# Second block: probabilities turned in 32x32 blocks too, turned operands kept in blocks of their own order, the three score units in one granule

## The reference

```
h = x @ w_in                          # q, k, v, z for 12 heads A and 12 heads B of 128, gates g
qa, ka = rope(qa), rope(ka)
out_a = mixture of three dilated causal windows over q, k, v (heads A)
out_b = softmax(q k' / sqrt(128) + D_t - D_s, causal) v      (heads B; D: summed log forget gates)
y = sigmoid(g_a) * ((out_a * silu(za)) @ w_up_a) + sigmoid(g_b) * ((out_b * silu(zb)) @ w_up_b)
x = layer_norm(x * alpha + y @ w_out)
```

## Time and profile before

| | |
|---|---|
| runs, median of 3 | 2801.91 us (2800.36 to 2802.63) |
| profiled execution | 2799.75 us |
| its span | 2798.0 us |
| mean granted TensorE clock | 0.994 |
| TensorE products / its weight loads | busy 99% / 81% of the span |
| VectorE, ScalarE, POOL | busy 65%, 48%, 13% |

### The profile page before, as it was taken

The page is one execution under the profiler, slowest core; times in us unless marked ns, Lnnn a source line. Parts: engine busy times, 40 slices in busy tenths (PEclk is TensorE's granted clock), DMA queues, the critical chain, the costliest instruction groups (busy, mean ns, idle before and its releaser), DMA issues.

```text
span 2798.0 us, 35964 instructions
## 1 busy us (share of the span) xinstructions
PE 2757.6 (99%) x13157; PEld 2253.2 (81%) x13157; DVE 1817.0 (65%) x2220; ACT 1346.3 (48%) x1765; POOL 370.9 (13%) x653
## 2 busy tenths in 40 slices
PE   8899999999999999999999999999999999999998
PEld 5477887888888888888888888888888888888886
DVE  7889899778657556655555556575565545555565
ACT  3255646556544453544444544444445444445443
POOL 0000010000001223100133100022131011331000
PEclk9999999999999999999999999999999999999999
DMA  9987798865655566566566566565566665665554
GB/s 397 414 311 241 272 342 307 309 222 190 215 194 181 188 201 205 185 220 196 191 202 203 191 196 223 181 195 187 191 203 205 208 199 183 206 206 187 193 213 148
DMA packets 178617, 622.74 MB, mean 223 GB/s; under 512 B 27688, under 2 KB 27984, under 8 KB 173088
## 3 DMA queue, kind: packets, MB, share of 16 engines
q1 hardware_dynamic: 155376, 583.08, 60.3%
q0 software_dynamic: 23088, 37.56, 4.6%
HBM read 599.51 MB, written 2.14 MB: 215 GB/s over the span
## 4 chain that ended last, share of the span: by engine, by line
PE 90%; DMA 4%; DVE 4%; ACT 1%; issue 0%; SPq 0%; DVEq 0%; ACTq 0%
PE acc L860 65%; PE acc L2455 16%; DMA raw<-in_w 2%; DVE wlo L1865 1%; PE psS L839 1%; PE psS L829 1%; DMA scr<-in_w_early 1%; PE psS L2455 1%; PE psS L2421 1%; PE psT L812 1%; PE psT L2378 1%; DMA mraw<-in_w_early 1%; DVE raw L1900 0%; PE psS L2440 0%; PE psT L2340 0%
## 5 line engine op out<-in xcount | busy, mean ns | idle before, releaser
L489 DVE TENSOR_TENSOR wlo<-raw,whi 128x1024 fp32r<-128x1024 f32 x670 | 819.4, 1224 | 783.7 <-ACT whi L372 782.0
L372 ACT ACTIVATE whi<-raw 128x1024 fp32r<-128x1024 f32 x670 | 708.9, 1059 | 980.3 <-PE acc L860 964.4
L860 PE MATMUL acc<-whi,tokens_hi 128*128 128x512 f32 x2304 | 632.3, 395 | 0.5 <-DVE tokens_lo L303 0.3
L860 PE MATMUL acc<-whi,tokens_lo 128*128 128x512 f32 x2304 | 618.2, 389 | 0.0
L860 PE MATMUL acc<-wlo,tokens_hi 128*128 128x512 f32 x2304 | 618.1, 389 | 0.0
L860 PEld LDWEIGHTS acc<-whi,tokens_lo 128*128 128x128 f32 x2304 | 432.4, 188 | 91.5
L860 PEld LDWEIGHTS acc<-wlo,tokens_hi 128*128 128x128 f32 x2304 | 432.4, 188 | 91.0
L860 PEld LDWEIGHTS acc<-whi,tokens_hi 128*128 128x128 f32 x2304 | 425.7, 188 | 85.6 <-DVE tokens_lo L303 0.9
L1564 ACT ACTIVATE whi<-raw 128x1024 fp32r<-128x1024 f32 x160 | 168.7, 1058 | 200.8 <-PE acc L2455 116.2
L1865 DVE TENSOR_TENSOR wlo<-raw,whi 128x1024 fp32r<-128x1024 f32 x160 | 195.3, 1223 | 82.2 <-ACT whi L1564 81.3
L2455 PE MATMUL acc<-whi,tokens_hi 128*128 128x512 f32 x800 | 226.1, 403 | 1.9 <-DVE tokens_lo L1974 1.2
(11 more groups left out here) (355 smaller groups left out, 2434.2 us busy)
## 6 DMA issues: line engine op xcount, KB each, us to landing
raw<-in_w SPq DMA_DIRECT2D x838, 512.0 KB, 4.2
raw<-in_w_late SPq DMA_DIRECT2D x80, 512.0 KB, 5.0
mraw<-in_w SPq DMA_DIRECT2D x64, 512.0 KB, 4.7
mraw<-in_w_late SPq DMA_DIRECT2D x48, 512.0 KB, 4.8
y<-in_w_early SPq DMA_DIRECT2D x12, 1024.0 KB, 15.4
mraw<-in_w_early SPq DMA_DIRECT2D x7, 1024.0 KB, 14.9
scr<-in_w_early SPq DMA_DIRECT2D x7, 1024.0 KB, 14.8
sgl<-in_w_early SPq DMA_DIRECT2D x6, 1024.0 KB, 15.0
```

Of the source, the lines that this page charges most:

```text
L372: act.activation(whi[:, n % SLOTS, :], raw[:, n % SLOTS, :], ACT.Copy).then_inc(s_hi, 1)
L489: dve.tensor_tensor(wlo[:, n % SLOTS, :], raw[:, n % SLOTS, :], whi[:, n % SLOTS, :].bitcast(F32), ALU.subtract).then_inc(s_lo, 1)
L860: m = pe.matmul(acc[c % 2][:, tb, :], a[:, kk, tb * P:(tb + 1) * P], b[:, n % SLOTS, k * CW:(k + 1) * CW], start=(kk == 0 and q == 0), sto ...
```

## The change

What it does:

- The `p` fills and their copies go. In step 33 (`R_PROB`) VectorE turns all 1536 columns of `prob` in 32x32 blocks into `pb`, which lies in the joint tile of `qT` and `kT`; POOL moves the blocks to `pT` (`probT`) with 16 more DMAs a group and a semaphore of its own (`s_pT`). The `o` units wait for these.
- The block turns write their blocks in an order in which the 32-partition pieces of a transfer are each one run of 1 KB (1.5 KB for the probabilities). `by_quad` keeps 32 neighbouring words together; `by_column` writes the words of a block's row 8 words apart (12 for the probabilities). The keys and the gated z take `by_quad`, the queries and the probabilities `by_column`. Each reader picks its words by the matching view: `turned_heads(kT)` for the moving keys, `queries(qT)` and `pT.rearrange(...)` for the stationary operands.
- The three score units stand in step 26: unit 2 as a fill in a `psT` bank, then units 0 and 1 in the `psS` banks. Both `o` units stand in step 37. VectorE's and ScalarE's score steps come one step earlier (29 to 31, 30 to 32), the `o` steps and `R_BLOCKS` one later (41, 42 and 43).
- The copies of the `heads` layout now cover z as well (`zheads`).

```diff
-R_BLOCKS = R_SCORES + 16
+R_PROB = R_SCORES + 7
+R_BLOCKS = R_SCORES + 17
 R_SPLIT = 50
 QUAD = 32
 QUADS = P // QUAD
+MOVED = 16 * QUADS * QUADS
...
-        if 0 <= r - R_SCORES - 5 <= 2:
-            out += [("p", grp, r - R_SCORES - 5)]
+        if r == R_SCORES:
+            out += [("s", grp, 2)]
...
-        if 0 <= r - R_SCORES <= 2:
-            out += [("s", grp, r - R_SCORES)]
-        if 0 <= r - R_SCORES - 10 <= 1:
-            out += [("o", grp, r - R_SCORES - 10)]
+        if r == R_SCORES:
+            out += [("s", grp, 0), ("s", grp, 1)]
+        if r == R_SCORES + 11:
+            out += [("o", grp, 0), ("o", grp, 1)]
...
-    qT = sb("qT", [P, HPG, SEQ])
-    kT = sb("kT", [P, HPG, SEQ])
+    qkT = sb("qkT", [P, 2 * HPG, SEQ])
+    qT, kT = qkT[:, 0:HPG, :], qkT[:, HPG:, :]
     v = sb("v", [P, TB, CW])
     z = sb("z", [P, TB, CW])
     prob = sb("prob", [P, 3, CW])
     probT = sb("probT", [P, 3, CW])
-    zb = prob[:, 0:TB, :].rearrange("p b (k t) -> p (b k) t", t=HD)
-    zT = probT[:, 0:TB, :].rearrange("p b (k t) -> p (b k) t", t=HD)
+    pT = probT[:].rearrange("p u n -> p (u n)")
+    pb = qkT[:].rearrange("p h t -> p (h t)")[:, 0:3 * CW]
+    zb = prob[:, 0:TB, :].rearrange("p b t -> p (b t)")
+    zT = probT[:, 0:TB, :].rearrange("p b t -> p (b t)")
     blocks = sb("blocks", [P, TB, CW])
     rtmp = blocks[:, 1, :]
-    heads = stage[:].rearrange("p b n -> p (b n)").rearrange("p (h b e) -> p b h e", b=TB, e=HD)
+    heads, zheads = (t[:].rearrange("p b n -> p (b n)").rearrange("p (h b e) -> p b h e", b=TB, e=HD)
+                     for t in (stage, z))
...
+    def by_feature(tile):
+        return tile.rearrange("p (k c j) -> p k c j", c=QUADS, j=QUAD)
+    def by_quad(tile):
+        return tile.rearrange("p (c k j) -> p k c j", c=QUADS, j=QUAD)
+    def by_column(tile):
+        return tile.rearrange("p (c j k) -> p k c j", c=QUADS, j=QUAD)
     def attended_views(grp):
 
         k = HPG * (grp % 3)
-        return [t[:, k:k + HPG, :].rearrange("p k (b t) -> p b k t", b=TB) for t in (ahi, alo)] + [
-            zT.rearrange("p (b k) t -> p b k t", b=TB)]
+        return [by_feature(t[:, k:k + HPG, :].rearrange("p k t -> p (k t)")) for t in (ahi, alo)] + [by_quad(zT)]
...
+            dst, src = (t.rearrange("p (c n) -> p c n", c=QUADS) for t in (dst, src))
             for b in range(QUADS):
                 for c in range(QUADS):
-                    pool.dma_start(dst[c * QUAD:(c + 1) * QUAD, :, b * QUAD:(b + 1) * QUAD],
-                                   src[b * QUAD:(b + 1) * QUAD, :, c * QUAD:(c + 1) * QUAD]).then_inc(signal, 16)
+                    pool.dma_start(dst[c * QUAD:(c + 1) * QUAD, b, :], src[b * QUAD:(b + 1) * QUAD, c, :])\
+                        .then_inc(signal, 16)
 
         def regrouped(l, grp):
 
             n = NGRP * l + grp
             for i, (dst, signal) in enumerate(((qT, s_qT), (kT, s_kT))):
-                pool.wait_ge(s_blk, 3 * n + i + 1)
-                if grp:
-                    pool.wait_ge(*unit_full(l, ("s", grp - 1, 2)))
-                elif l:
-                    pool.wait_ge(*unit_full(l - 1, ("s", NGRP - 1, 2)))
-                blocks_moved(dst[:].rearrange("p h (b t) -> p (h b) t", b=TB),
-                             blocks[:].rearrange("p b (k t) -> p (b k) t", t=HD), signal)
-            pool.wait_ge(s_blk, 3 * n + 3)
+                pool.wait_ge(s_blk, 4 * n + i + 1)
+                if n:
+                    pool.wait_ge(s_pT, MOVED * n)
+                blocks_moved(dst.rearrange("p h t -> p (h t)"), blocks[:].rearrange("p b t -> p (b t)"), signal)
+            pool.wait_ge(s_blk, 4 * n + 3)
             if n:
                 pool.wait_ge(s_alo, n)
+            blocks_moved(pT, pb, s_pT)
+            pool.wait_ge(s_blk, 4 * n + 4)
             blocks_moved(zT, zb, s_zT)
...
-            def fill_copy(name, dst):
-                act.wait_ge(*filled(l, name))
-                act.activation(dst, bank_t(name)[:], ACT.Copy).then_inc(s_tfree[FILL2[name] % 2], 1)
...
-                if 0 <= r - R_SCORES - 5 <= 2:
-                    u = r - R_SCORES - 5
+                if 0 <= r - R_SCORES - 4 <= 2:
+                    u = r - R_SCORES - 4
...
-                if 0 <= r - R_SCORES - 9 <= 2:
-                    u = r - R_SCORES - 9
-                    if u == 0 and NGRP * l + grp:
-                        act.wait_ge(s_alo, NGRP * l + grp)
-                    fill_copy(("p", grp, u), probT[:, u, :])
                 if r == R_SCORES + 12:
                     if NGRP * l + grp:
-                        act.wait_ge(s_blk, 3 * (NGRP * l + grp))
-                    evacuate(c0 + 3, z, ACT.Silu)
+                        act.wait_ge(s_blk, 4 * (NGRP * l + grp))
+                    evacuate(c0 + 3, zheads, ACT.Silu)
...
-                dve.transpose(blocks[:].rearrange("p b n -> p (b n)"), stage[:].rearrange("p b n -> p (b n)"))\
+                    dve.wait_ge(s_qT, MOVED * (NGRP * l + grp + 1))
+                dve.transpose((by_column, by_quad)[which](blocks[:].rearrange("p b n -> p (b n)")),
+                              by_feature(stage[:].rearrange("p b n -> p (b n)")))\
                     .then_inc(s_blk, 1)
...
-                if 0 <= r - R_SCORES - 4 <= 2:
-                    u = r - R_SCORES - 4
+                if 0 <= r - R_SCORES - 3 <= 2:
+                    u = r - R_SCORES - 3
                     name = ("s", grp, u)
-                    bank = UNIT2[name] % 2
+                    if u < 2:
+                        bank, full, free = psS[UNIT2[name] % 2], unit_full(l, name), s_sfree[UNIT2[name] % 2]
+                        read = unit_read(l, name)
+                    else:
+                        bank, full, free = bank_t(name), filled(l, name), s_tfree[FILL2[name] % 2]
+                        read = copied(l, name)
...
+                if r == R_PROB:
+                    dve.wait_ge(s_exp, at(l, 3 * NGRP, 3 * grp + 3))
+                    dve.transpose(by_column(pb), by_feature(prob[:].rearrange("p u n -> p (u n)"))).then_inc(s_blk, 1)
...
-                if 0 <= r - R_SCORES - 14 <= 1:
-                    tb = r - R_SCORES - 14
+                if 0 <= r - R_SCORES - 15 <= 1:
+                    tb = r - R_SCORES - 15
...
-                        dve.wait_ge(s_zT, 16 * QUADS * QUADS * n)
-                    dve.transpose(zb.rearrange("p a t -> p (a t)"), z[:].rearrange("p b n -> p (b n)")).then_inc(s_blk, 1)
+                    dve.wait_ge(s_blk, 4 * n + 3)
+                    dve.transpose(by_quad(zb), by_feature(z[:].rearrange("p b n -> p (b n)"))).then_inc(s_blk, 1)
...
+            def turned_heads(tile):
+                return tile.rearrange("p h t -> p (h t)").rearrange("p (c h t j) -> p h t c j", c=QUADS, h=HPG, t=TB)
+            def queries(tile):
+                return tile.rearrange("p h t -> p (h t)").rearrange("p (t h b) -> p h b t", h=HPG, b=TB)
+            def scores(name, bank):
+                _, grp, u = name
+                pe.wait_ge(s_qT, MOVED * (NGRP * l + grp + 1))
+                pe.wait_ge(s_kT, MOVED * (NGRP * l + grp + 1))
+                w, tb = (P, 0) if u == 0 else (SEQ, 1)
+                for b in range(CW // w):
+                    h = b + max(0, 2 * (u - 1))
+                    m = pe.matmul(bank[:, b * w:(b + 1) * w].rearrange("p (t c j) -> p t c j", c=QUADS, j=QUAD),
+                                  queries(qT)[:, h, tb], turned_heads(kT)[:, h, 0:tb + 1], start=True, stop=True)
+                return m
...
-                    pe.wait_ge(s_exp, at(l, 3 * NGRP, 3 * name[1] + name[2] + 1))
-                    for k in range(4):
-                        t = pe.transpose(bank[:, k * P:(k + 1) * P], prob[:, name[2], k * P:(k + 1) * P], ident[:])
+                    t = scores(name, bank)
...
-                    for p in ((0,), (1, 2))[tb]:
-                        pe.wait_ge(*copied(l, ("p", grp, p)))
+                        pe.wait_ge(s_pT, MOVED * (NGRP * l + grp + 1))
                     for h in range(HPG):
                         for s in range(tb + 1):
                             u, col = (0, h) if tb == 0 else (1 + h // 2, 2 * (h % 2) + s)
-                            m = pe.matmul(bank[:, h * HD:(h + 1) * HD], probT[:, u, col * P:(col + 1) * P],
+                            m = pe.matmul(bank[:, h * HD:(h + 1) * HD], pT.rearrange("p (t k) -> p k t", k=3 * HPG)[:, HPG * u + col],
```

More of the change, by code:

```diff
@@ L216, in second_block @@
     s_kT = sem("c_kT")
+    s_pT = sem("c_pT")
     s_zT = sem("c_zT")
@@ L396, in evacuate @@
                 src = acc[c % 2][:]
-                if dst is heads:
+                if dst is not v:
                     src = src.rearrange("p b (h e) -> p b h e", e=HD)
@@ L403, in attention @@
                 if grp >= 3 and r == R_Q - 2:
-                    act.wait_ge(s_blk, 3 * (NGRP * l + grp) - 1)
+                    act.wait_ge(s_blk, 4 * (NGRP * l + grp) - 2)
                     evacuate(c0, heads, ACT.Copy, SCALE2)
```

(56 more changed lines are left out.)

## The result

The changed kernel takes 2851.31 us (median; 2849.59 to 2853.20) against 2801.55 before: a ratio of 1.0179, 95% interval 1.0167 to 1.0191. It is 49.8 us slower. The forecast was 2828 with a range to 2850: the direction held, the range did not, and the loss is nearly twice the 26 us of the sum.

What follows compares the result with a forecast made beforehand. TensorE's issues were taken to bound the kernel: -17.5 us for turns removed, +43.5 for doubled loads, 0 for the rest, +26.0 us on 2799.75, giving 2825.8 and, with 2.2 for the runs' median, 2828 us; 8-in-10 range 2782 to 2850.

Steps and rivals of the forecast that it cites:

- Bound and unit of account: Second block: time is the sum of TensorE's issues; a plain granule of 12 products takes 2.72 us, any excess prices an insertion.
- Turns removed, -17.5 us: 144 turned tiles (36 `p` fills) leave TensorE, gained in full: 17.5 us less.
- Entering and leaving an insertion costs nothing: Score and `o` units on TensorE: excesses are whole multiples of a pass, so merging units saves 0.
- No cover for a load: Loads of 128 neighbouring words take about 114 ns, a 128-column pass; nothing hides slower ones in 32 of 40 passes a group.
- The doubling, +43.5 us: Stationary operands of score and `o` units: a load with gaps takes 227 ns instead of 114, 43.5 us in all; chance 0.50.
- the figure of VectorE: 2.50 against 1.05 ns a column for gapped writes; by that 2.4 ratio a TensorE load would take 272 ns, 65 us.
- Late landings, cost 0, bound 6 us: `o` unit 0 in step 37 waits for the probabilities' 16 DMAs: 2.2 us slack or about none; cost 0, at most 6 us.
- a turn slowed by gaps: VectorE's turn of the probabilities at doubled cost, 3.7 us: POOL's first issue comes 20.6 us after step 26 starts.
- the likeliest case: Loads slowed 1.6 to 2.4 times, with or without late landings: 2828 us, own range 2812 to 2850, chance 0.50.
- VectorE, POOL's queue, ScalarE's copies: VectorE's extra turn is covered by idle time, POOL's 16 more issues a group fit, ScalarE's removed copies gain nothing: 0 us.
- Loads with gaps are no slower: Rival for TensorE's stationary loads: gaps fit the spare half of the stream rate, -17.5 us, 2784 us; chance 0.34.
- about none: Slack before step 37 on TensorE for the probabilities' landing if VectorE's turn doubles: 31.3 to 33.1 against 32.64 us.

Runs made afterwards that it cites:

- plain_early: Changed kernel with neighbouring words for queries and probabilities and VectorE's turn of the probabilities one step earlier (32 for 33): 2782.27 us, ratio 0.9938.
- before_gaps: Kernel before, only TensorE's stationary operands read with gaps (queries every 8th word, probabilities every 4th): 2844.40 us, ratio 1.0155.
- gaps_early: Changed kernel, all gaps kept, VectorE's turn of the probabilities one step earlier (32 for 33): 2841.73 us, ratio 1.0144.
- cut_p: Changed kernel with the probabilities' DMAs cut from 48 to 32 KB each from the second group on, same number and start: 2842.18 us, ratio 1.0148.
- plain_both: Changed kernel with queries and probabilities stored so that TensorE's stationary operands are 128 neighbouring words: 2793.39 us, ratio 0.9973.

## Why the prediction was wrong

- *Bound and unit of account.* Right: TensorE's issues make up the time, and from step 26 of the first group on its terms give the whole difference: -17.5 + 57.4 + 12.5 = 52.4 us.
- *Turns removed, -17.5 us.* Right: plain_early shows 17.9, and the 0.1 us a group of the merged units is in it. "Entering and leaving an insertion costs nothing" was off by that much.
- *No cover for a load.* Right. The reading of the earlier trace rows, a load just as long as a 128-column pass, is what before_gaps shows: a slower load is paid in 32 of 40 passes, all but part of the first load of a unit (eight score passes take 1.70 us to the next product's start, where eight at the 238 ns of every 8th word would take 1.90).
- *The doubling, +43.5 us.* This step failed, by its size; the mechanism was right. "I take the doubling" is true of a gap of 4 words (before_gaps, 44.4 us). The new layouts have 8 and 12: the loads of the `o` units take 267 ns, 2.36 times, and those of the score units some 240 by 3.86 us over 16 passes. Without waits the term is 12 x (1.13 + 3.65) = 57.4 us, 3.65 being the 6.35 of gaps_early less 2.70. The rows gave no way to tell 2.0 from 2.4; the figure of VectorE in the Trainium skill ("Vector Engine (DVE) Microarchitecture Reference", section 5.2) gave 65 us for it, nearer than mine, and I had left it in a sentence beside the sum. That it came near is luck as far as these runs show: VectorE's own turn with a gap of 12 words took 1.7 times as long, not 2.4.
- *Late landings, cost 0, bound 6 us.* Failed as well: 12.5 us, of which 8.6 stand in the table of waits, 1.9 are what the table leaves out, and 2.0 are the restarts. The landing was the wrong term: I used the 2.1 to 3.9 us of a 32 KB transfer for one of 48 KB, and it took up to 5.7; with 32 KB at the same place it took up to 4.4 (cut_p, second group). Scaled by the bytes, 3.9 would have been 5.9. That the start came out right, 21.1 us after step 26 for the 20.6 of a turn slowed by gaps, is two errors that cancel in part: step 26 was 1.1 us longer than counted, the turn took 2.98 us of the 3.7 allowed. POOL's issues also took 7.3 us from first to last where I had 8.6, since its long pieces go faster. Without these two savings the landings would have been 2 us later in every group.
- *The range.* The price of the gap alone would have stayed in it: gaps_early, without late landings, takes 2841.7 us. The landings took the result over 2850. And the likeliest case was said to run to 2.4 times "with or without late landings", but its end of 2850 has room for one of them only: 2.4 times and 6 us of landings give 2799.75 + 2.2 - 17.5 + 65 + 6 = 2855.
- *VectorE, POOL's queue, ScalarE's copies.* Beyond the wait for the probabilities nothing of theirs showed in TensorE's waits. Right.
- *The rivals.* "Loads with gaps are no slower" fell with before_gaps. Its price, 2784, is what the kernel gives when the gaps are gone.

What is open: why 4, 7, 8, 9, 11 and 12 words cost the stationary operand more than 5, 6 and 10, when none shares a 16-byte stretch with the next. That leaves the step from 2.0 to 2.4 times, on which the size of the loss rests, measured but not explained.

## What to carry to other kernels

A layout made for the DMAs is paid for by its readers. Before storing an operand with gaps, compare the pass with the load: where the moving operand is as short as the stationary one, nothing hides a slower load. In these runs pairs of neighbouring words, or every second word, kept a read within 6% of full speed. When a step's slack comes out as "about none", take the landing of a transfer of the same bytes, and move the step.

## What the runs showed of the hardware

- The price of a gap for TensorE, fp32, 24 passes of 128 columns. Stationary operand: 1.06 times at every 2nd word, 1.6 at every 3rd, 2.1 at every 4th, 2.0 to 2.4 up to every 12th. Moving operand: 1.03, 1.5, 2.0, and 2.0 up to every 8th; runs of 2 or 4 words free.
- A wait of TensorE for a DMA right before such passes costs more than its length: 0.17 us at a gap of 12 words (gaps_early against the changed kernel).
- VectorE's block turn writing with gaps of 12 words takes 2.98 us for 1536 words; with neighbours:

```profile
L672 DVE STREAM_TRANSPOSE qkT<-prob x12: 1771/1772/1772, 937.6 to 2529.8; 128x1536 f32<-128x1536 f32 x12
```

  1.77 us, so 1.7 times.
- POOL's time for an issue grows with the number of pieces. In plain_both the probabilities' DMAs have 12 x 32 pieces of 128 bytes, the z DMAs 32 of 1 KB:

```profile
L351 POOL DMA_DIRECT2D probT<-qkT x192: 615/617/645, 939.7 to 2541.0; - x192
L343 POOL DMA_DIRECT2D probT<-prob x192: 498/498/517, 969.5 to 2569.6; - x192
```

  617 against 498 ns, and 583 for 8 x 32 pieces in the earlier trace rows. The long pieces were worth 16 x 85 ns = 1.4 us of POOL's time a transfer of q, k or z, and could not pay for the reads.
